# The context stream of the second block, moved into blocks of 12 to 15 steps between the expert passes of the first block

## The reference, cut to what matters

```python
# first block: x is [256 tokens, 1024]
for l in range(2):
    mod = silu(c) @ w_ada[l] + b_ada[l]                  # 6 x 1024 (shift, scale, gate, twice)
    mix = even_mixer(u) if l == 0 else odd_mixer(u)      # projections, attention heads, output projection
    x = layer_norm(alpha * x + (1 + g1) * mix)
    f = hierarchical_moe(u)                              # 32 experts of 6 MB, top 2 per token
    x = layer_norm(alpha * x + (1 + g2) * f)
# second block: h = x, hc = ctx (256 context tokens)
for i in range(2):                                       # i = 0: window attention, i = 1: neighbourhood attention
    mod, mod_c = silu(c) @ w_ada_2[i] + ..., silu(c_ctx) @ w_ada_2[i] + ...
    a, ac = modulate(h, g_mix[i], ...), modulate(hc, g_mix[i], ...)      # rms norm, scale, shift
    y, yc = mixer(a, ac)                                 # x attends to its keys and to those of ac; ac to itself
    h = h + gt1 * y
    h = h + gt2 * swiglu(modulate(h, g_ffn[i], ...))     # 1024 -> 2 x 2816 -> 1024
    if i == 0:
        hc = hc + gt1c * yc
        hc = hc + gt2c * swiglu(modulate(hc, ...))
```

## Time and profile before

| what | value |
|---|---|
| time, 3 runs | 2847.42 us median (2846.04 to 2847.89) |
| profiled execution | 2847.75 us, span 2845.7 us, mean granted TensorE clock 0.927 |
| TensorE matmul busy | 2334.1 us (82%) |
| TensorE weight load busy | 1297.5 us (46%) |
| VectorE busy | 755.3 us (27%) |
| ScalarE busy | 427.0 us (15%) |
| loaded from memory | 618.53 MB, 218 GB/s over the span |
| expert loads | 360 of 1 MB each (192 and 168) |
| chain that ended last | PE 65%, DMA 19%, DVE 9%, issue 3%, ACT 2% |

### The profile page before, as it was taken

One profiled execution on the slowest core, in us unless ns is written; L12 is line 12 of the kernel. 1 busy time (PEld: TensorE's weight loads), 2 busy tenths in 40 slices (PEclk: granted clock), 3 DMA queues, 4 the chain that ended last, 5 costly groups with the idle time before them and its releaser, 6 DMA issues.

```text
span 2845.7 us, 25830 instructions
## 1 busy us (share of the span) xinstructions
PE 2334.1 (82%) x10178; PEld 1297.5 (46%) x10178; DVE 755.3 (27%) x1875; ACT 427.0 (15%) x1065; POOL 27.9 (1%) x42
## 2 busy tenths in 40 slices
PE   6987477766669866777665999999999999988999
PEld 3656233322237453343222455444444445447888
DVE  1144321111120841122113578210010023582010
ACT  1021100000011311000002246120000011162000
POOL 0000000000000000000000000000000000030000
PEclk8998798989789878999888999999999999999999
DMA  9680889899973619889996136012122212122330
GB/s 400 261 362 1 328 345 392 372 421 421 421 313 148 266 54 422 341 339 421 421 421 261 59 148 237 30 59 89 59 89 85 78 59 89 59 75 89 148 133 15
DMA packets 86627, 621.22 MB, mean 218 GB/s; under 512 B 10000, under 2 KB 10160, under 8 KB 11504
## 3 DMA queue, kind: packets, MB, share of 16 engines
q1 hardware_dynamic: 83952, 611.36, 53.0%
q0 software_dynamic: 1984, 5.02, 0.7%
q10 hardware_dynamic: 576, 3.25, 0.3%
HBM read 618.53 MB, written 1.05 MB: 218 GB/s over the span
## 4 chain that ended last, share of the span: by engine, by line
PE 65%; DMA 19%; DVE 9%; issue 3%; ACT 2%; SPq 1%; DVEq 0%; ACTq 0%
PE bank L596 64%; DMA ring<-in_moe_w 18%; DVE scratch L1451 2%; SPq L530 1%; DMA ring<-in_w_ada 1%; DVE tiny L1905 1%; ACT work L1111 1%; ACT u L1111 1%; DVE zmore L1919 1%; ACT res L1111 0%; PE bank L988 0%; DVE tiny L1934 0%; ACT scratch L1111 0%; DVE adaT L1392 0%; DVE u L1915 0%
## 5 line engine op out<-in xcount | busy, mean ns | idle before, releaser
L596 PE MATMUL bank<-u,ring 128*128 128x256 f32 (+1 forms) x2912 | 895.0, 470 | 53.7 <-ACT u L1111 39.2
L596 PEld LDWEIGHTS bank<-u,ring 128*128 128x128 f32 x2912 | 564.1, 194 | 378.6 <-issue 300.1
L596 PE MATMUL bank<-ring,work 128*32 128x512 f32 (+2 forms) x2880 | 496.8, 730 | 256.1 <-DMA ring<-in_moe_w 222.2
L596 PEld LDWEIGHTS bank<-ring,work 128*32 128x32 f32 (+2 forms) x2880 | 156.0, 137 | 570.3 <-issue 564.7
L596 PE MATMUL bank<-work 128*128 128x128 f32 (+3 forms) x1280 | 253.8, 351 | 41.3 <-ACT work L1111 18.4
L1111 ACT ACTIVATE work<-bank 128x512 f32<-128x512 f32 (+2 forms) x155 | 83.2, 538 | 1254.1 <-PE bank L596 948.3
L596 PEld LDWEIGHTS bank<-work 128*128 128x128 f32 (+1 forms) x1280 | 183.1, 190 | 107.7 <-issue 52.2
L596 PE MATMUL bank<-work,ring 128*128 128x512 f32 (+1 forms) x704 | 227.5, 486 | 2.8 <-DVE work L1981 2.8
L596 PEld LDWEIGHTS bank<-work,ring 128*128 128x128 f32 x704 | 133.6, 190 | 96.7 <-issue 87.7
L1451 DVE RECIPROCAL scratch<-scratch 128x512 f32<-128x512 f32 (+1 forms) x40 | 113.3, 2832 | 104.1 <-ACT scratch L1111 104.1
L1981 DVE TENSOR_TENSOR work<-work,bank 128x512 f32<-128x512 f32 (+1 forms) x44 | 24.4, 554 | 428.6 <-PE bank L596 428.6
(11 more groups left out here) (211 smaller groups left out, 1309.3 us busy)
## 6 DMA issues: line engine op xcount, KB each, us to landing
ring<-in_moe_w SPq DMA_DIRECT2D x360, 1024.0 KB, 18.2
ring<-in_w_ada SPq DMA_DIRECT2D x96, 1024.0 KB, 9.7
ring<-in_w_gate_up SPq DMA_DIRECT2D x44, 1024.0 KB, 6.6
ring<-in_w_down SPq DMA_DIRECT2D x22, 1024.0 KB, 5.0
ring<-in_even_w_in SPq DMA_DIRECT2D x14, 1024.0 KB, 9.5
ring<-in_odd_w_in SPq DMA_DIRECT2D x12, 1024.0 KB, 20.1
ring<-in_na_w_qkv SPq DMA_DIRECT2D x12, 1024.0 KB, 4.8
ring<-in_swa_w_qkv SPq DMA_DIRECT2D x6, 1024.0 KB, 20.0
```

The lines of the kernel that those rows point to most:

```text
L596: return pe.matmul(o, l, r, start=start, stop=stop, skip_group_check=True)
```

## The change: what it does

The context's whole way through the second block becomes one list of steps, `context_steps()`. Each step has one to three small tiles of 256 columns and its own PSUM banks (5, 6, 7 in turn); x keeps banks 0 to 4 in the expert stages and all eight elsewhere. `CTX_PLAN` and `MOE_PLAN` say how many steps stand at which point. A string of `MOE_PLAN` is one pass, its nine places are: behind the gather, phases 0 to 3, the transposes, phases 4 and 5, the scatter ("s"). So the first layer runs 15, 15, 14 and 12 steps behind passes 1, 3, 5 and 7 and 8 behind the gather of pass 8; the second 14, 12, 12, 12 and 6. The first two steps stand in the even mixer, eight in the first layer's norm and routing, two behind its last norm, eight in the second layer's norm and routing.

The steps by block: key and value tiles, five head norms, heads 0 to 4 | heads 5 to 19 (with their tails) | 8 output tiles, statistics, gates 0 to 3 | ups, downs, gates 4 to 7 | ups, downs; second layer: the rest of the gated layer in chunks of four, statistics, keys and values for the neighbourhood attention.

The context reads its own copies of the weights, 256 columns to a load: 51 more loads of 1 MB, 18 in the first expert stage and 24 in the second. The panels of layer 2 move from the odd mixer into the even one, those of layer 3 from the window attention into the odd mixer, four panels of layer 1 forward into the input projections. GpSimd loads the context behind the retention's scores. The second block has x alone: one stream everywhere, no padded keys (a matmul on 64 partitions instead), the context's keys and values from `ckv`, `res[:, 1]` and `u[:, 1]`.

```diff
+CTX_PLAN = {"even": 2, "ln0a": 2, "route0a": 2, "route0b": 4, "ln0b": 2, "ln1a": 2, "route1a": 2, "route1b": 4}
+MOE_PLAN = (("00000000f", "000000000", "00000000f", "000000000", "00000000e", "000000000", "00000000c", "800000000"),
+            ("00000000e", "000000000", "00000000c", "000000000", "00000000c", "000000000", "00000000c", "600000000"))
...
+X_BANKS, CTX_BANKS, ALL_BANKS = (0, 1, 2, 3, 4), (5, 6, 7), tuple(range(8))
...
+def context_steps():
+    steps = [("sq", 0), ("rms", 0)]
+    steps += [("q", i) for i in range(8)] + [("k", 0), ("k", 1), ("v", 0), ("v", 1)]
+    steps += [("nrm", 0), ("nrm", 1), ("swap", 0)] + [("nrm", j) for j in range(2, 5)]
+    steps += [("head", n) for n in range(HQ + 4)]
+    steps += [("out", i) for i in range(8)] + [("sq", 1), ("rms", 1)]
+    for c in range(CHUNKS):
+        n = range(4 * c, min(4 * c + 4, FFT))
+        steps += [("gate", i) for i in n] + [("up", i) for i in n] + [("down", 4 * c + j) for j in range(4)]
+    steps += [("sq", 2), ("rms", 2)]
+    for p in range(4):
+        steps += [("k3", 2 * p), ("k3", 2 * p + 1)] + [("nrm3", p - 1)] * (p > 0)
+    steps += [("v3", 0), ("nrm3", 3)] + [("v3", i) for i in range(1, 8)]
+    return steps
...
             for i, ranks in enumerate(PASS_RANKS):
+                ctx_jobs(l, i, "g")
                 for ph in range(6):
...
+                    ctx_jobs(l, i, ph)
+                    if ph == 3:
+                        ctx_jobs(l, i, "t")
+                ctx_jobs(l, i, "s")
...
             ada_jobs(0, 4 + g, 5 + g)
+            if g >= 3:
+                ada_jobs(1, g - 3, g - 2)
...
+        ada_jobs(1, 10, 12)
+        job("adafin1a", 1)
+        job("adafin1b", 1)
+        job("retO", 4)
+        ada_jobs(2, 0, 2)
+        job("retM", 2)
+        ada_jobs(2, 2, 4)
+        job("adafin2a", 1)
+        job("retV", 2)
+        ada_jobs(2, 4, 8)
+        ctx_jobs("even")
+        ada_jobs(2, 8, 12)
+        job("out0.0", 4, panel(a["even_w_out"][0], 0))
+        job("adafin2b", 1)
+        job("out0.1", 4, panel(a["even_w_out"][0], 1))
...
+            def context_tile(kind, i):
+                w = context_weights(kind, i)
+                at = P * (i % 2)
+                one_tile(ctile[kind, i], lambda o: [
+                    (o[:, 0:S], w[:, k, at:at + P], uc[:, k], k == 0, k == KT - 1) for k in range(KT)])
...
+            def ctx(*point):
+                for kind, i in points[point]:
...
+                    elif kind == "nrm":
+                        pe.wait_ge(c_nsq, i + 1)
+                        one_tile(ctile[kind, i], lambda o: [(o[:, :], K("blk64"), cnsq(i))])
+                    elif kind == "swap":
+                        pe.wait_ge(c_nrm, 1)
...
+                    elif kind == "head":
+                        if i == 0:
+                            pe.wait_ge(c_nrm, 5)
...
-                for c, b in enumerate((7, 4, 0, 1)):
+                for c, b in enumerate((1, 2, 3, 0)):
                         for k in range(2):
                             n_ = 2 * c + k
                             r = mm(bank[b][:, S * k:S * k + S], ysb[:, P * n_:P * n_ + P], selT)
                         r.then_inc(m["scattered"], 1)
+                    ctx("s")
...
-                streams = 2 if L == 2 else 1
-                rhs = u_in(U_N[L][1], streams)
-                width = S * streams
+                rhs = u_in(U_N[L][1])
                 for g in range(11):
-                    project(f"gu{L}.{g}", rhs, width)
+                    project(f"gu{L}.{g}", rhs, S)
```

More of the change, by code:

```diff
@@ L122, in shape_constants @@
     put("quad", quad)
[L123 to L126, removed]
+    put("swap", np.roll(np.eye(P), 64, 1))
     put("iota", np.arange(P)[None, :])
@@ L283, in build @@
+        hidden = W(0, FFT, S)
         pT = X(0, 4, 4, S)
[L284 to L293, removed]
+        zbuf = {2: [W(4096 + 512 * i, 512) for i in range(6)], 3: [W(6144 + 512 * i, 512) for i in range(6)]}
@@ new lines, in build, with new_tile, x_banks, new_load @@
+        last_in, used = [None] * 8, [0] * 8
+        def new_tile(b):
+            t = state["t"]
+            bank_of.append(b)
+            ahead.append(last_in[b])
+            used[b] += 1
+            nth.append(used[b])
+            last_in[b] = t
+            state["t"] += 1
+            return t
+        def x_banks(banks):
+            state["x"], state["at"] = banks, 0
+        def new_load(src, rel):
+            r = state["n"] % RING
+            per_pos[r] += 1
+            loads.append((r, per_pos[r], src, rel))
+            state["n"] += 1
@@ new lines, in ctx_plan, with ctx_tile, ctx_jobs @@
+        def ctx_plan(*point):
+            if len(point) == 1:
+                return CTX_PLAN.get(point[0], 0)
+            l, i, at = point
+            at = ("g", 0, 1, 2, 3, "t", 4, 5, "s").index(at)
+            return int(MOE_PLAN[l][i][at], 16)
+        def ctx_tile(name, i):
+            ctile[name, i] = new_tile(CTX_BANKS[state["ctx"] % len(CTX_BANKS)])
+            state["ctx"] += 1
+        def ctx_jobs(*point):
+            n = ctx_plan(*point)
+            points[point], todo[:n] = todo[:n], []
+            for kind, i in points[point]:
+                if kind == "head":
+                    if i < HQ:
+                        ctx_tile("S", i)
+                    if i % 2 == 0 and 4 <= i < HQ + 4:
+                        ctx_tile("O", (i - 4) // 2)
+                    if 2 <= i < HQ + 2:
+                        ctx_tile("T", i - 2)
+                elif kind != "sq":
+                    ctx_tile(kind, i)
+                key, src = context_sources(kind, i)
+                if key:
+                    if key not in cslot:
+                        cslot[key] = len(loads)
+                        new_load(src, ("context", key))
+                    clast[key] = ctile[kind, i]
@@ L330, in expert_jobs @@
             moe_end.append(len(loads))
+            assert all(isinstance(v[2], tuple) for v in loads[-RING:])
         def down_jobs(L):
@@ L1099, in _ @@
             ln_sums("ln0b", 2)
+            ctx("ln0b")
             odd()
@@ L1260, in rms @@
                     act.wait_ge(cent_done, cnt["cent"])
[L1261 to L1263 removed]
+                    f(u[:, 0, k], u[:, 0, k], ACT.Identity, bias=mod[:, L, 24 * half + k, 0:1]).then_inc(u_act, 1)
             def head_norms(L):
@@ L1952, in attention @@
+                    step(dve.reciprocal(sm[:, 11:12], sm[:, 10:11]))
+                    ts(z, z, sm[:, 11:12], None, ALU.mult).then_inc(soft_p, 1)
+                for n in range(HQ + 4):
+                    for qb in range(2):
+                        if n < HQ:
+                            shift(2 * n + qb)
+                    for qb in range(2):
+                        if 1 <= n <= HQ:
+                            norm(2 * (n - 1) + qb)
                     if n >= 5 and n % 2 == 1:
                         pair = (n - 5) // 2
-                        s, h = UNITS[L][2 * pair]
@@ L1983, in second @@
-                add_second(L, [T(f"down{L}", k) for k in range(8)], 40, streams)
+                    tt(hidden[:, n], hidden[:, n], B(t)[:, 0:S], ALU.mult).then_inc(moved[bank_of[t]], 1)
+                add_second(L, [T(f"down{L}", k) for k in range(8)], 40)
             even()
```

1029 lines of the change are left out of this document (641 added, 388 removed).

## The result

Before, 2847.13 us median of 12 runs (2846.04 to 2848.68); changed, 2854.93 us median of 12 (2852.14 to 2857.74). The ratio is 1.0026, 95% interval 1.0017 to 1.0035: slower by a quarter of a percent, where 2829 us, 0.65% faster, was forecast. The profiled execution has a span of 2855.9 us at a mean granted clock of 0.91.

A forecast was written before the change was run, and what follows sets the result against it. Bounds: a serial engine chain with ring-depth waits in passes two to six, the DMA queue from the seventh, TensorE in the second block. 2845.7 - 443.6 + 45 + 211 + 169 = 2827.1 us of span, so 2829; range 2787 to 2870.

The forecast's parts named there:

- start to the end of the first pass: Program start: panels and loads delay the first output projection, and context tiles delay routing; +40 us.
- first expert stage: First layer's experts: context blocks of steps between passes lengthen the path, less small waits absorbed; +211 us.
- from there to the second stage's first pass: Between the expert stages: gate tiles behind the first layer's end and context tiles in routing; +5 us.
- second expert stage: Second layer's experts: context blocks cost 179.7 us, less 3.5 and 7.4 covered or absorbed; +169 us.
- second block: Layers after the experts, on x alone: projections, attentions, gated layer and statistics get cheaper; -443.6 us, bounds 430 and 455.
- 37: Start: net delay of the first output projection by panels and loads, 267 against 227 less moved sums; bounds 10 and 45.
- 11 heads and a tail, between both: 49: First expert stage, block of 15 attention steps: 7.2 to 9.1 us per two heads, 49 us; bounds 30 and 60.
- A mask addition per unit more: 72: Second block, window attention: neighbourhood attention's 80.2 us has an extra mask addition per unit, so 72 us, from 126.8.
- the 10.1: Second block, statistics ahead of the window projections: 20.7 us falls to 10.1 with one stream.
- rival 1: Expert stages: waits for loads absorb the context blocks; 2783 us, chance 0.12.
- Rival 2: Norm and attention blocks: the clock falls and stays down into the work behind them; 2864 us, chance 0.18.
- Rival 3: Start hides its loads better, the ring running ahead during stick-breaking heads; 37 falls to 15, 2807 us, chance 0.08.

The follow-up runs named there:

- run 4: Changed kernel with eight of layer 2's twelve modulation panels moved from the start to behind the fourth pass of the first expert stage: 2867.3 us.
- run 5: Changed kernel with VectorE copying a context pair's output tile at the head of its next attention step, before that step's maximum and scaling: 2829.8 us.
- run 6: Changed kernel with each score matmul of the context's 16 heads run twice: 2870.8 us.
- run 9: Changed kernel with unread filler matmuls cut to wait length: six ahead of the neighbourhood attention, three or one before the attentions' first transposes: 2846.3 us.
- run 7: Changed kernel with unread filler matmuls in waits: ten ahead of the neighbourhood attention, six before the first transposes of both second-block attentions: 2850.5 us.
- run 2: Changed kernel with context matmul tiles in pairs ahead of the fourth and sixth phases of four-expert passes, the rest behind passes: 2763.2 us.
- run 3: Changed kernel with tiles paired inside four-expert passes, and attention and first-layer norm steps placed one by one: 2697.6 us.
- run 8: Kernel of run 3 with a third tile pair per four-expert pass moved ahead of the fifth phase, and VectorE's early output copy: 2653.7 us.
- run 11: Kernel of run 8 with eight layer 2 modulation panels moved from the start, one by one behind context heads in one-expert passes: 2649.6 us.

## Why the prediction was wrong

The mechanism stood: the end is cheaper by the context's work, the expert stages dearer by nearly the same, and the waits for loads absorb little. The gain, a difference of two sums near 430, was lost in the sizes of three terms. Measured less forecast, on the span, of 28.8 us in all:

| term | forecast | measured | differs by |
| --- | --- | --- | --- |
| start to the end of the first pass | +40 | +46.0 | +6.0 |
| first expert stage | +211 | +223.5 | +12.5 |
| from there to the second stage's first pass | +5 | +1.7 | -3.3 |
| second expert stage | +169 | +169.4 | +0.4 |
| second block | -443.6 | -430.4 | +13.2 |

- **Start.** The projection came at 269.7 for 267. From there the forecast took off nearly 3 us for the sums of layer 1 that leave, net of one that comes; by its own rows these are 1.7 less 0.9. Also left out: the projection begins at a lower clock behind waits for loads (16.94 us for its first half, 14.03 for the second). So "37" measured 44. Run 4 shows that 24 of the 42 us by which the projection starts later belong to eight of the panels, their loads and their matmuls together.
- **First stage, the step that failed most: the price of the attention block.** "11 heads and a tail, between both: 49" measured 60.3, above its bound of 60 and 11.3 of the stage's 12.5 us; the other blocks came within 2.1 us of their forecasts (52.9 for 53, 53.6 for 51.5, 42.6 for 42). The latency per two heads was put at 7.2 to 9.1 us; it is 10.3, since VectorE's copy of an output tile stands behind the next head's maximum and scaling, and with three banks the transposes wait for it. I named the wait of a score tile for its bank and missed this one. Runs 5 and 6 show that this wait, not the work, also keeps the clock down; without it the block takes 37.1 us, 12 under the forecast. The Trainium skill, "TensorE: Matmul & The Clock Gate", "A second HAM failure mode: psum-queue depth-cycling", says that short idles of TensorE between groups, as it cycles through accumulator banks, make the clock oscillate. The trace agrees (0.62 in the block, 0.95 without the bank's wait).
- **Second block.** "A mask addition per unit more: 72" was the wrong bound: it takes work off VectorE, but TensorE sets the pace at 8.48 us per two heads, and the first heads run at half clock. 81.4 measured; at a clock of 0.98 it takes 75.0 (run 9), so 6.4 of the 9.4 are the clock and the waits that the fillers stand in, and 3 are the pace of the loop. The neighbourhood attention, taken as unchanged, took 3.6 more (83.8 for 80.2). Behind its 4.7 us wait it ran at half clock for its first 24 us, against 0.90 in the first 31 before; with the clock at 0.98 it took 78.9 (run 7), so the clock can account for it. The statistics ahead of the window projections took 2 more than the 10.1.
- **The waits for loads.** The third and fifth passes of both layers wait 53.5 us where they waited 55.2: rival 1 is out. Of the 29 us that went, 18 lie in the seventh and eighth passes, where 15 had been counted, and 9 in the first passes, where none had. Runs 2, 3 and 8 show why so little went: what a wait can absorb must stand inside the pass, between the phase that gives a slot back and the phase that waits for it.
- **Rival 2** (the clock) was right in kind: 2864 was worked out, 2855 came. It hit the attention block and the attention stages, and the tiles behind a statistics step by some 2 us (15.92 us for four, against 13.98). It spared the starts of the blocks (7.07 us for their first two tiles, the full clock), where most of the 15 us had been put. Rival 3 is out.
- **The range** held the time (2787 to 2870); the chances, 0.64 for faster, leaned on a gain (18.6 us) smaller than the errors of its terms (28.8 in all, nearly all one way). That the time fell inside the range is no sign that the terms were right.

## What to carry to other kernels

Work that is to fill waits must be put between what frees the buffers and what waits for them; the same work in blocks between the passes costs nearly its full time (2855 us), in pairs inside them it made the kernel 7% faster (2654). Part of such a gain is the clock: from the changed kernel to run 8 TensorE's busy time fell by 75 us with the same matmuls, its idle time by 121. Where a gain is the difference of two large sums, read the new loop's slowest chain, bank by bank, before believing it. Loads moved off a crowded start came back as waits where sixteen stood in one place (run 4); one panel at a time, in a stretch with queue to spare, they did not (run 11), though what that gained in all is within the noise.

## What the hardware showed unexpectedly

- A loop of small matmuls with one 2.4 us wait per 10 us had a granted clock of 0.62 (0.59 from its fourth head on); the same loop with 1.2 us waits per 5.5 us had 0.95; and with twice the score matmuls and the 2.4 us wait kept, 0.50.
- One wait of 2.3 to 4.7 us in or ahead of an attention stage was followed by 14 to 24 us at half clock (16 behind 2.29 us and 24 behind 4.68 in the changed kernel, 14 behind 2.48 in run 9), though the gaps in these stretches were under 1 us. With the wait filled the same heads ran at 0.93 to 1.00 (run 7).
- A pass with 64 rows of contraction and 256 columns starts 0.22 us behind the one before (0.43 for two, in the lines of the changed kernel below), as one with 128 rows does (3.62 us for 16): 64 rows instead of padded keys take no less of TensorE. Whether two such passes on different rows would run side by side was not tried.

```profile
2054.37 0.59 PE L760 MATMUL bank<-work 64*128 64x256 f32 x2
2054.81 0.59 PE L760 MATMUL bank<-ckv,work 64*128 64x256 f32 x2
```
